# Growing the delta rule's triangular inverse in 32-row blocks instead of 64-row blocks, with the transposed copy made on VectorE

## Chip, cores and metric

The kernel runs on one core of a Trainium2 chip. The metric is the device time of one execution in microseconds (us), start to end; lower is better. Inputs and outputs are float32.

## What is computed

The reference is a two-layer mixer followed by two layers of a second kind. Each layer of the first kind has an attention branch and a gated delta rule branch; the change touches the delta rule alone:

```python
def chunked_gated_delta_rule(q, k, v, beta, g):
    ...
    lower = jnp.where(strict, jnp.einsum('bhnid,bhnjd->bhnij', kb, k) * decay, 0.0)
    tmat = jnp.eye(CHUNK, dtype=jnp.float32) + lower
    u = lax.linalg.triangular_solve(tmat, v * beta[..., None], left_side=True,
                                    lower=True, unit_diagonal=True)
    w = lax.linalg.triangular_solve(tmat, kb * jnp.exp(gc)[..., None], left_side=True,
                                    lower=True, unit_diagonal=True)
    ...
```

With 8 heads, 256 positions and 128 columns per head, each layer solves with unit lower triangular matrices I + L. The kernel uses blocks of 128 positions, so there are 2 x 8 matrices of 128x128 in a layer, and it computes their inverses explicitly.

## The kernel before

All five engines run one static program. A list of steps, `PLAN`, is merged from several lanes by the string `ORDER` (L319): one letter takes the next step of that lane. Lane `a` holds the delta rule's chain, `b` the attention chain, `m` the big matrix products, `s` the loading and splitting of weights, and others hold drains and tails. Every engine goes through `PLAN` from the front and does its part of each step, so `ORDER` fixes the order of work on each engine; semaphores make a step wait for its inputs.

The bulk of the work are products with weights (`mm`, L941, L926, L934): a weight unit of 512 KB comes in by DMA, ScalarE rounds it to a high part (`w_hi`, L1347), GpSimd subtracts to get the low part (`w_lo`, L866, L868), and TensorE forms three products. One unit of two K blocks is 12 matmuls of 128x512. Steps of the chains stand between such units on TensorE, and their results go to two PSUM buffers `chain`, used in turn; a step that takes a buffer waits until the step before the last has been emptied.

The delta rule runs in two groups `g` of four heads in each layer, so four inverses of 8 matrices each (2 row blocks, 4 heads) are made in a run. In each:

- `rep` (TensorE, L1053) and `sub` (VectorE, L1958 to L1973) invert the 8x8 diagonal blocks and write them, transposed, into 64-wide rows of `xth`.
- `x1` (TensorE, through `half_blocks`, L970) transposes them by products with the identity, and ScalarE copies the result into `xh`. Both the inverse so far (`xh`) and its transpose (`xth`) are kept.
- For each of the levels 8, 16, 32: `invY` multiplies with L (16 matmuls of 64x64x64, L970), VectorE masks the result (L1999); `invZ` forms the correction and, as a second product, its transpose (32 matmuls, L970), and VectorE subtracts the one from `xh` (L2006, step `invZ`) and the other from `xth` (L2015, or L2018 and L2019 at the last of the three, step `invX`).
- Level 64 joins the two 64-row halves: 8 matmuls (L1080), a copy (L1996), 8 matmuls (L1095), a subtraction (L2009).
- `vT` turns the values (8 transposes, L962); it stands behind `invZ` of the first level and is independent of the inverse. `raw` (L1143) and `iT` (L962) are steps of the attention chain.

The matmuls of the first three levels come in pairs, one on rows 0 to 63 and one on rows 64 to 127 of the array:

```python
for j in range(R * 4):
    for at in halves:
        a, b = pair(j, at)
        m = pe.matmul(c[at, col + j * HALF:col + (j + 1) * HALF], a, b, ...)
```

The trace shows two matmul instructions for each such float32 matmul, so the 160 of an inverse are 320 instructions, and 1280 in the run. All of a product's results lie in one PSUM bank, 512 float32 per partition.

Of the kernel before, what the change touches and what calls it, by code (L numbers as in the profile page):

```python
# [29 lines left out]
P = 128  # L30
# [23 lines left out]
HALF = P // 2  # L54
K_ID, K_TRIU, K_LEVEL, K_BLOCK, K_NEG, K_STR, K_NSTR, K_TRIL, K_ONE, K_FREQ, K_UNIT, K_LATER, K_HALF, K_OWN = (
    0, 128, 256, 448, 576, 832, 1088, 1344, 1472, 1600, 1640, 1648, 1776, 1777)
K_COLS = K_OWN + HALF


def shape_constants():  # L60
# [5 lines left out]
    own = HALF * (p // HALF) + f[:, 0:HALF]  # L66
    for n, s in enumerate(LEVELS[:-1]):
        c[:, K_LEVEL + n * HALF:K_LEVEL + (n + 1) * HALF] = (
            (p // (2 * s) == own // (2 * s)) & (p // s % 2 == 1) & (own // s % 2 == 0))
    c[:, K_BLOCK:K_BLOCK + P] = p // BLK == f // BLK  # L70
    c[:, K_OWN:K_OWN + HALF] = p // BLK == own // BLK
# [163 lines left out]
def gdn_chain(g):  # L235
    out = [("stat", 0, g), ("stat", 1, g), ("rn", g), ("avT", g),
           ("dec", g, 0), ("dec_b", g, 0), ("dec_c", g, 0), ("kk", g, 0), ("dec", g, 1), ("dec_b", g, 1),
           ("dec_c", g, 1), ("kk", g, 1), ("rep", g), ("sub", g), ("x1", g)]
    for n in range(len(LEVELS)):
# [4 lines left out]
        if n < len(LEVELS) - 1:  # L244
            out.append(("invX", g, n))
        if n == 0:
            out.append(("vT", g))
# [51 lines left out]
def lanes():  # L299
# [20 lines left out]
    "aaaaasammssvamsmssaamaaasaacsccasscccssammcmmsmaacssmmaacssccsmmmamaaasasmdabsmaaabssmmcsmaammassdbm"  # L320
    "adbmssaaammsssammsbadamsabaamamsaaaamssacmasccmaamasbsbbmacccscmammssmsccsaacbcmmbssmambbsaaasssammb"
    "bdsaaaamsssdmmmmaassdwbbssmmmsamcbmmamssssbbdbbmmaaambabxxsasbmaabbbsddmxssbaamswwamaaamaassmamsdwaa"
    "mwbasxsxmmsdmsaxbmwxsaxxxbmbbmxaxvsvsssmssmmmammsmaammsdsaaammsssssvammmmaaaascasscmmsccasscmcassccm"
    "msmaammcmsacsmcasmsassdaaaammasassmmaambbsmambacmaaamdassmssbdbssmaamabammaaamssaaadmsscamacsmssssaa"
    "mmamccacccmssbbscbcmmcamssacammbbsssmabbsmaaamdssaaaammssdsammadmmaabbscbbbmaswmmssdsbbbaassmsssmaaw"
    "maabmmbambsbxmxxbmssdbbbmmsssdamawammaasaadswwmbamasxxbsamaamssbaxdbbwxsxxmmmxxxsssssvsmmsvasadmmmmm"
    "mmsaaaasassaassmmdsssssdssbsdsbbmmmmmmsmmmmammmmsssaassdaasmmbbsaadbbsmmmbsaaasmmbddabbmbbmssaaamvba"
    "bmbsssddmmbbadmmsssybbmbssbmaambdsymsbamdsyyavbymbysydvvmmyssdmvssvvvvdmsvvvdmmmmssdymmmmmmvvvssssss"
    "yvvsmmmmmmmvmmmvsseeessvvvvaeeessmmaaammmbmmmmmmssdmssssssssdmmmmmadsasmsbaaammmbbbaassdasssdbbmbmma"
    "asaamsbmbsddbmbbmaaabmsssvbbmbasmmsabbdmbddsssasmabbssmymmambayddssmbsmbdsssydvyysmsdbsyyvvmmydmmmmv"  # L330
    "svsmdvvvvmsvvyssssmmvvvmmyvvmvvmssemmmmmsseemmvvvveemmme"
# [3 lines left out]
def plan():  # L335
# [17 lines left out]
    "kk": "vector", "rep": "vector", "x1": "scalar", "kT": "vector", "invY": "vector", "invZ": "vector", "vT": "vector",  # L353
# [13 lines left out]
def emptied_by(step, *args):  # L367

    if step == "invZ" and args[-1] < len(LEVELS) - 1:
        return "invX"  # L370
    return EMPTIED_BY.get(step, step)
# [96 lines left out]
def build(nc, t, out):  # L468
    ctx = ExitStack()
    with ctx:  # L470
# [68 lines left out]
        xh, yh, xth = xx8[:, :, 0:HALF], yy8[:, :, 0:HALF], yy8[:, :, HALF:P]  # L539
# [336 lines left out]
        def _(pe):  # L876
            def handlers(p):
# [1589 lines left out]
```

## Time and profile before

| | |
|---|---|
| median of 3 runs | 1063.06 us (1062.7 to 1064.39) |
| span of the profiled execution, first to last instruction | 1056.6 us |
| the profiled execution's own time | not listed apart; the three runs lie 6.1 to 7.8 us above the span |
| TensorE busy | 1025.6 us, 97% of the span, 7112 matmuls |
| VectorE, ScalarE, GpSimd busy | 57%, 55%, 67% |
| bytes moved | 151.59 MB, 143 GB/s on the mean |

The page says for each engine how long it was busy, and for the 40 slices of the span how busy. The views by line give the duration of an operation, the views of waits tell which engine stood still for which, and the chain that ended last tells in order of time which work set the end. A matmul's end is modelled and matmuls overlap, so what one costs is read from the distance of starts, or from groups of different length.

### The profile page before, as it was taken

Reading aid. Unit: us, or ns where it says so; the run is one execution under the profiler, and the core shown is the slowest. Engines: PE = TensorE matmul, PEld = TensorE weight load, DVE = VectorE, ACT = ScalarE, POOL = GpSimd, SP = SyncE. Lnnn points to the kernel's source line nnn. Section 1 sums busy time; section 2 is a strip of 40 time slices with the busy share of each in tenths; the row PEclk is TensorE's granted clock in tenths of the full one; section 3 lists DMA queues with packets and bytes.
Section 4 is the critical chain, followed back from the end, with each engine's and each line's share of the span. In section 5 each row is a group of like instructions: output and inputs, shape, how many; then the busy total and the mean of one; then the engine's idle time right before and its main releaser. Section 6 shows DMA issues by size and latency. Waiting matters only on the chain.

```text
span 1056.6 us, 18561 instructions
## 1 busy us (share of the span) xinstructions
PE 1025.6 (97%) x7112; PEld 886.4 (84%) x7112; DVE 599.0 (57%) x1181; ACT 577.4 (55%) x968; POOL 712.2 (67%) x550
## 2 busy tenths in 40 slices
PE   8999999999999999999999998999999989999986
PEld 8988998888877988899888887788888768888875
DVE  4774366786565557246584563517446560646564
ACT  4754347656644574336656744445576534567652
POOL 4786537872648787556766645897366978744794
PEclk9999999999999999999999999999999999999999
DMA  8664434653425555435444332665233546423451
GB/s 294 192 179 122 139 101 131 173 156 107 134 100 153 180 165 157 140 84 157 141 139 141 115 125 87 209 191 158 81 113 120 186 140 216 133 91 108 140 183 57
DMA packets 80584, 151.59 MB, mean 143 GB/s; under 512 B 6448, under 2 KB 12400, under 8 KB 80496
## 3 DMA queue, kind: packets, MB, share of 16 engines
q1 hardware_dynamic: 80496, 150.41, 46.9%
q8 instruction: 57, 0.93, 0.4%
q14 instruction: 31, 0.25, 0.1%
HBM read 149.34 MB, written 1.05 MB: 142 GB/s over the span
## 4 chain that ended last, share of the span: by engine, by line
PE 88%; DVE 4%; ACT 3%; POOL 3%; issue 2%; DMA 0%; POOLq 0%; SPq 0%; DVEq 0%; ACTq 0%
PE bulk L941 53%; PE bulk L926 12%; PE chain L962 5%; PE chain L970 4%; PE chain L1039 4%; PE chain L1307 1%; PE bulk L934 1%; PE chain L1288 1%; ACT arena L1347 1%; PE chain L1163 1%; PE chain L1179 1%; POOL w_lo L868 1%; DVE arena L1846 1%; PE chain L1030 1%; POOL w_lo L866 1%
## 5 line engine op out<-in xcount | busy, mean ns | idle before, releaser
L866 POOL TENSOR_TENSOR w_lo<-raw,w_hi 128x512 fp32r<-128x512 f32 (+3 forms) x259 | 340.7, 1316 | 292.4 <-ACT w_hi L1347 291.8
L868 POOL TENSOR_TENSOR w_lo<-raw,w_hi 128x512 fp32r<-128x512 f32 (+3 forms) x277 | 375.6, 1357 | 31.8 <-ACT w_hi L1347 31.8
L1347 ACT ACTIVATE w_hi<-raw 128x1024 fp32r<-128x1024 f32 (+4 forms) x277 | 277.3, 1019 | 210.1 <-PE bulk L941 163.4
L941 PE MATMUL bulk<-w_hi,hT_hi 128*128 128x512 f32 (+1 forms) x756 | 306.0, 405 | 0.8 <-ACT arena L1347 0.5
L941 PE MATMUL bulk<-w_hi,hT_lo 128*128 128x512 f32 (+1 forms) x756 | 294.4, 389 | 0.0
L941 PE MATMUL bulk<-w_lo,hT_hi 128*128 128x512 f32 (+1 forms) x756 | 204.2, 389 | 1.9 <-POOL w_lo L868 1.9
L941 PEld LDWEIGHTS bulk<-w_hi,hT_hi 128*128 128x128 f32 x756 | 142.4, 188 | 33.5 <-issue 1.9
L941 PEld LDWEIGHTS bulk<-w_lo,hT_hi 128*128 128x128 f32 x756 | 141.7, 188 | 32.7 <-POOL w_lo L868 3.4
L941 PEld LDWEIGHTS bulk<-w_hi,hT_lo 128*128 128x128 f32 x756 | 142.5, 188 | 26.8 <-issue 1.0
L926 PE MATMUL bulk<-hT_hi,w_hi 128*128 128x256 f32 x384 | 96.3, 289 | 0.0
L926 PE MATMUL bulk<-hT_lo,w_hi 128*128 128x256 f32 x384 | 94.0, 282 | 0.0
L962 PE MATMUL chain<-cst,arena 128*128 128x128 f32 (+1 forms) x544 | 73.4, 276 | 7.8 <-DVE arena L2223 3.5
L962 PEld LDWEIGHTS chain<-cst,arena 128*128 128x128 f32 (+1 forms) x544 | 62.7, 142 | 15.1 <-issue 9.3
L926 PEld LDWEIGHTS bulk<-hT_hi,w_hi 128*128 128x128 f32 x384 | 73.4, 191 | 0.9 <-ACT w_hi L1347 0.7
L1347 ACT ACTIVATE arena<-chain 128x512 f32<-128x512 f32 (+4 forms) x64 | 45.5, 727 | 52.0 <-PE chain L962 23.6
L926 PEld LDWEIGHTS bulk<-hT_lo,w_hi 128*128 128x128 f32 x384 | 73.5, 191 | 0.0
L1846 DVE SCALAR_TENSOR_TENSOR arena<-bulk,par,arena 128x253 f32<-128x253 f32 (+2 forms) x144 | 59.4, 475 | 21.0 <-ACT arena L1347 19.0
L1342 ACT ACT_TABLE_LOAD x44 | 56.5, 1283 | 26.5 <-PE bulk L941 14.3
L1347 ACT ACTIVATE arena<-bulk 128x1024 f32<-128x1024 f32 (+2 forms) x50 | 50.1, 1006 | 17.3 <-PE bulk L941 17.2
L926 PE MATMUL bulk<-hT_hi,w_lo 128*128 128x256 f32 x384 | 53.9, 283 | 0.0
L1347 ACT ACTIVATE arena<-arena,tiny 128x256 f32<-128x256 f32 (+1 forms) x80 | 36.2, 454 | 27.0 <-DVE tiny L2345 19.4
L926 PEld LDWEIGHTS bulk<-hT_hi,w_lo 128*128 128x128 f32 x384 | 49.5, 192 | 0.0
(262 smaller groups left out, 1393.4 us busy)
## 6 DMA issues: line engine op xcount, KB each, us to landing
raw<-in_w_in_dram SPq DMA_DIRECT2D x194, 512.0 KB, 3.6
raw<-in_w_out_dram SPq DMA_DIRECT2D x32, 512.0 KB, 3.7
raw<-in_w_branch_dram SPq DMA_DIRECT2D x16, 512.0 KB, 3.7
raw<-in_w_mem_kv_dram SPq DMA_DIRECT2D x8, 512.0 KB, 3.4
raw<-in_w_merge_up_dram SPq DMA_DIRECT2D x16, 256.0 KB, 2.9
raw<-in_w_in_dram SPq DMA_DIRECT2D x8, 420.0 KB, 3.4
gain<-in_ln_rows_dram SPq DMA_DIRECT2D x4, 512.0 KB, 5.3
gain<-in_gains_dram SPq DMA_DIRECT2D x3, 512.0 KB, 6.1
```

Of the source, the lines that this page charges most:

```text
L866: pool.tensor_tensor(lo_of(p, u)[:, 0:at], raw_of(p, u)[:, 0:at], hi_of(p, u)[:, 0:at].bitcast(F32), ALU.subtract).then_inc(first_part, 1)
L868: pool.tensor_tensor(lo_of(p, u)[:, at:n], raw_of(p, u)[:, at:n], hi_of(p, u)[:, at:n].bitcast(F32), ALU.subtract).then_inc(p.done("split" ...
L926: m = pe.matmul(dst, part[:, k, j * P:(j + 1) * P], b[:, kk, :], start=(not low and kk == 0 and i == 0 and j % 2 == 0), stop=(low and kk = ...
L934: m = pe.matmul(pair[0:n, 0:S], part[:, k, :], b[:, kk, :], start=(not low and kk == 0 and i == 0), stop=(low and kk == tot - 1))
L941: m = pe.matmul(dst, a, part[:, k, :], start=(first and not low and k == 0 and i == 0), stop=(last and low and k == nk - 1))
L962: m = pe.transpose(c[0:n, i * P:i * P + v.shape[0]], v, ident[0:v.shape[0], 0:v.shape[0]])
L970: m = pe.matmul(c[at, col + j * HALF:col + (j + 1) * HALF], a, b, start=(j == 0), stop=(j == R * 4 - 1), skip_group_check=True)
L1030: pe.matmul(c[:, j * P:(j + 1) * P], spread(4 * r + j, 8), rows_T[0:8, :], start=(j == 0), stop=(j == 3), skip_group_check=True)
L1039: m = pe.matmul(c[:, j * P:(j + 1) * P], a, b, start=(j == 0), stop=(j == 3), skip_group_check=True)
L1342: act.preload_act_table_set(sets[func])
L1347: return act.activation(dst, src, func, **more)
L1846: ins = STT(cv[:, j, back:S], b[:, j * S:(j + 1) * S - back], par1[:, p.l, c:c + 1], cv[:, j, back:S], ALU.mult, ALU.add)
```

## The change

The inverse now grows in 32-row blocks up to level 32, and the transposed copy comes from VectorE:

- `half_blocks` becomes `quad_blocks`: for each of the 8 matrices four matmuls of 32x32x32 on the four 32-row blocks of the array. All results lie in one bank as before, 32 columns for each matrix (256 in all, not 512).
- `sub` writes 32-wide rows with one operation for all 8 matrices, and VectorE's transpose of 32x32 blocks makes the other copy. `x1` is gone from TensorE and ScalarE.
- At levels 8 and 16, `invZ` forms one product; VectorE subtracts, and then transposes the result (`invX`).
- A new VectorE step `place` spreads the 32-row blocks into the 128-wide and 64-wide matrices, zero elsewhere, by two multiplications with a mask.
- Level 32 is now a joining step: the tiles take their weights from one 32-row block and write the neighbouring one; both products are formed, and VectorE writes them with the sign changed. Level 64 is as before.
- `ORDER` is another string (as many letters). Loads, splits and all other products are the same steps in another order.

```diff
-                def half_blocks(c, pair, col=0):
+                def quad_blocks(c, pair, to=0, col=0):
 
                     for j in range(R * 4):
-                        for at in halves:
-                            a, b = pair(j, at)
-                            m = pe.matmul(c[at, col + j * HALF:col + (j + 1) * HALF], a, b, start=(j == 0), stop=(j == R * 4 - 1),
+                        for i in range(4):
+                            at, dst = quads[i], quads[i ^ to]
+                            a, b = pair(j, at, dst)
+                            m = pe.matmul(c[dst, col + j * QUAD:col + (j + 1) * QUAD], a, b, start=(j == 0), stop=(j == R * 4 - 1),
                                           skip_group_check=True)
...
-                def x1(g):
-                    c = take("x1", g)
-                    pe.wait_ge(*p.after("vector", "sub", g))
-                    half_blocks(c, lambda j, at: (xth[at, j, :], ident[at, at])).then_inc(p.done("x1"), 1)
...
-                    if n < len(LEVELS) - 1:
-                        half_blocks(c, lambda j, at: (lt8[at, j, at], xh[at, j, :])).then_inc(p.done("invY"), 1)
+                    if LEVELS[n] < QUAD:
+                        m = quad_blocks(c, lambda j, at, dst: (lt8[at, j, at], xq[at, j, :]))
+                    elif LEVELS[n] == QUAD:
+                        m = quad_blocks(c, lambda j, at, dst: (lt8[at, j, dst], xq[at, j, :]), to=1)
...
-                    if n < len(LEVELS) - 1:
-                        half_blocks(c, lambda j, at: (xth[at, j, :], yh[at, j, :]))
-                        half_blocks(c, lambda j, at: (yh[at, j, :], xth[at, j, :]), 512).then_inc(p.done("invZ"), 1)
+                    if LEVELS[n] < HALF:
+                        m = quad_blocks(c, lambda j, at, dst: (xtq[at, j, :], yq[at, j, :]))
+                        if LEVELS[n] == QUAD:
+                            m = quad_blocks(c, lambda j, at, dst: (yq[at, j, :], xtq[at, j, :]), to=1, col=512)
...
-                    for r in range(R):
-                        for j in range(4):
-                            ins = TT(xth[:, 4 * r + j, :].rearrange("p (b i) -> p b i", i=BLK),
-                                     over(inv[:, 4 * r + j, :], HALF // BLK), blocks, ALU.mult)
-                    ins.then_inc(p.done("sub"), 1)
+                    TT(xtq_flat.rearrange("p (m b i) -> p m b i", m=R * 4, i=BLK), inv[:, :, :].unsqueeze(2).broadcast_to(dims),
+                       blocks.unsqueeze(1).broadcast_to(dims), ALU.mult).then_inc(p.own, 1)
+                    v.wait_ge(*p.last())
+                    v.transpose(xq_flat, xtq_flat).then_inc(p.done("sub"), 1)
...
+                    if LEVELS[n] < QUAD:
+                        v.transpose(xtq_flat, xq_flat).then_inc(p.done("invX"), 1)
...
+                def place(g):
+
+                    own = cst[:, K_QUAD:K_QUAD + 4]
+                    for dst, src, n, at in ((xt8, xtq, 4, slice(0, P)), (xh, xq, 2, halves[0])):
+                        dims = [at.stop, R * 4, n, QUAD]
+                        ins = TT(dst[at, :, :].rearrange("p m (b n) -> p m b n", b=n), src[at, :, :].unsqueeze(2).broadcast_to(dims),
+                                 own[at, 0:n].unsqueeze(1).unsqueeze(3).broadcast_to(dims), ALU.mult)
+                    ins.then_inc(p.done("place"), 1)
```

In layer 0, group 0, TensorE had this order from `x1` to `invZ` of the first level (`iT`'s 5 transposes and `vT`'s 8 are L962; the leading rows of bulk units are left out):

```order
L970 MATMUL chain<-cst,arena 64x64 x16
...
L970 MATMUL chain<-arena 64x64 x16
L962 MATMUL chain<-cst,arena 128x128 x5
...
L941 MATMUL bulk<-w_lo,hT_hi 128x512 x4
L970 MATMUL chain<-arena 64x64 x32
L962 MATMUL chain<-cst,arena 128x128 x8
L941 MATMUL bulk<-w_hi,hT_hi 128x512
```

At the same place it now has `invY`, one bulk unit, `invZ`, `vT` and at once `invY` of the second level:

```order
L980 MATMUL chain<-arena 32x32 x32
L950 MATMUL bulk<-w_hi,hT_hi 128x512
...
L950 MATMUL bulk<-w_lo,hT_hi 128x512 x4
L980 MATMUL chain<-arena 32x32 x32
L971 MATMUL chain<-cst,arena 128x128 x8
L980 MATMUL chain<-arena 32x32 x32
```

`x1` is gone, the second product of `invZ` is gone, and between `invZ` and the next `invY` only `vT`'s 8 transposes are left, where two bulk units stood behind them.

On VectorE, in the same inverse, the first two levels and the start of the third were (L1986 drains `vT`):

```order
L1999 TENSOR_TENSOR arena<-chain,cst 128x8x64
L2006 TENSOR_TENSOR arena<-arena,chain 128x8x64
L2015 TENSOR_TENSOR arena<-arena,chain 128x8x64
L1986 TENSOR_TENSOR arena<-chain,tiny 128x512 x2
L1999 TENSOR_TENSOR arena<-chain,cst 128x8x64
```

and are now:

```order
L2006 TENSOR_TENSOR arena<-chain,cst 128x256
L2013 TENSOR_TENSOR arena<-arena,chain 128x256
L2024 STREAM_TRANSPOSE arena<-arena 128x256
L1991 TENSOR_TENSOR arena<-chain,tiny 128x512 x2
...
L2036 TENSOR_TENSOR arena<-arena,cst 128x1024
L2036 TENSOR_TENSOR arena<-arena,cst 64x512
L2003 COPY arena<-chain 128x256
```

The subtraction of the second copy became a transpose of half the columns, and `place` (L2036) stands between the second and third level, once in each inverse.

## Rows read from the trace of the kernel before

**Rows 1.** The page: busy time of each engine; granted TensorE clock in 40 slices.
```profile
PE 1025.6 (97%) x7112; PEld 886.4 (84%) x7112; DVE 599.0 (57%) x1181; ACT 577.4 (55%) x968; POOL 712.2 (67%) x550
...
PEclk9999999999999999999999999999999999999999
```

**Rows 2.** Windows: stretch, length, busy time by engine, clock, DMA share, GB/s.
```profile
core 0: us, PE busy (x) PEld busy (x) DVE busy (x) ACT busy (x) POOL busy (x), PEclk, DMA share, GB/s
50.00:150.00 100.00, 99.98 (x916) 87.52 (x914) 52.96 (x138) 44.97 (x74) 63.40 (x51) 1.00 0.47 138
516.00:636.00 120.00, 118.57 (x918) 100.53 (x917) 77.88 (x165) 71.72 (x125) 76.13 (x58) 1.00 0.45 132
```

**Rows 3.** Waits: who waited for whom, us in total, times, longest; ScalarE, GpSimd, TensorE.
```profile
POOL w_lo L866 <- ACT w_hi L1347: 291.8, 110, 13.0
ACT w_hi L1347 <- PE bulk L941: 163.4, 102, 5.3
...
PE chain L962 <- DVE arena L2223: 3.5, 2, 2.9
```

**Rows 4.** The chain that ended last, 86 to 120 us: start, us, what, instructions.
```profile
87.81 1.08 PE chain L970 x32
88.89 2.95 PE bulk L941 x12
...
96.36 2.01 PE chain L970 x64
98.37 1.02 PE chain L962 x8
99.40 5.48 PE bulk L941 x24
...
118.34 1.09 PE chain L1143 x16
```

**Rows 5.** TensorE's timeline: 64-row tiles in pairs (L970) and one alone (L1080).
```profile
112.11 2.08 PE L970 MATMUL chain<-arena 64*64 64x64 f32 x64
117.19 1.15 PE L970 MATMUL chain<-arena 64*64 64x64 f32 x32
...
124.51 1.11 PE L1080 MATMUL chain<-arena 64*64 64x64 f32 x16
```

**Rows 6.** TensorE's timeline: pairs of 8-row tiles with 128 columns.
```profile
63.59 0.27 PE L1030 MATMUL chain<-arena,cst 8*128 8x128 f32 x1
63.60 0.27 PE L1032 MATMUL chain<-arena,cst 8*128 8x128 f32 x1
63.70 0.27 PE L1030 MATMUL chain<-arena,cst 8*128 8x128 f32 x1
```

**Rows 7.** Groups by line, VectorE: shapes xcount, busy us, mean ns, idle before.
```profile
L2223 DVE TENSOR_TENSOR arena<-arena 128x1024 f32<-128x1024 f32 x4 | 5.9, 1466 | 0.5
L1999 DVE TENSOR_TENSOR arena<-chain,cst 128x512 f32<-128x512 f32 x12 | 8.3, 692 | 26.4 <-PE chain L970 26.3
L2242 DVE CUSTOM_DVE_ANT_0 arena<-arena 128x384 f32<-128x384 f32 (+1 forms) x8 | 7.9, 1041 | 58.6 <-ACT arena L1347 58.6
L2353 DVE TENSOR_TENSOR arena<-chain,tiny 128x256 f32<-128x256 f32 x12 | 5.1, 424 | 0.4
L2351 DVE RECIPROCAL tiny<-tiny 128x4 f32<-128x4 f32 x12 | 2.1, 178 | 28.6 <-PE chain L1307 28.5
```

**Rows 8.** VectorE's timeline in `sub` of layer 0, group 0: first and last operations.
```profile
82.47 0.22 DVE L1965 TENSOR_TENSOR chain<-chain,tiny 128x56 f32<-128x56 f32 x1 [2.07 <-PE chain L1053]
...
85.46 0.17 DVE L1968 TENSOR_TENSOR tiny<-tiny,chain 128x8 f32<-128x8 f32 x1
85.66 1.29 DVE L1973 TENSOR_TENSOR arena<-tiny,cst 128x64 f32<-128x64 f32 x8
```

**Rows 9.** VectorE's timeline: the handover from TensorE to `invZ`'s subtraction.
```profile
98.49 0.69 DVE L2006 TENSOR_TENSOR arena<-arena,chain 128x512 f32<-128x512 f32 x1 [4.76 <-PE chain L970]
```

**Rows 10.** Groups by line: ScalarE's table loads, GpSimd's second half of a split.
```profile
L868 POOL TENSOR_TENSOR w_lo<-raw,w_hi 128x512 fp32r<-128x512 f32 (+3 forms) x277 | 375.6, 1357 | 31.8 <-ACT w_hi L1347 31.8
...
L1342 ACT ACT_TABLE_LOAD x44 | 56.5, 1283 | 26.5 <-PE bulk L941 14.3
```

More of the change, by code:

```diff
@@ L237, in gdn_chain @@
            ("dec", g, 0), ("dec_b", g, 0), ("dec_c", g, 0), ("kk", g, 0), ("dec", g, 1), ("dec_b", g, 1),
-           ("dec_c", g, 1), ("kk", g, 1), ("rep", g), ("sub", g), ("x1", g)]
+           ("dec_c", g, 1), ("kk", g, 1), ("rep", g), ("sub", g)]
     for n in range(len(LEVELS)):
@@ L245, in gdn_chain @@
             out.append(("invX", g, n))
+        if LEVELS[n] == QUAD // 2:
+            out.append(("place", g))
         if n == 0:
@@ L319 @@
 ORDER = (
[L320 to L329, printed above, removed]
@@ L352 @@
     "baT": "vector", "memT": "vector", "cwT": "vector", "hT": "vector", "gc": "vector", "stat": "scalar", "dec": "vector", "avT": "scalar",
-    "kk": "vector", "rep": "vector", "x1": "scalar", "kT": "vector", "invY": "vector", "invZ": "vector", "vT": "vector",
+    "kk": "vector", "rep": "vector", "kT": "vector", "invY": "vector", "invZ": "vector", "vT": "vector",
     "kq": "vector", "u": "scalar", "st": "scalar", "ks": "vector", "o": "vector", "iT": "scalar",
@@ L367, in emptied_by @@
 def emptied_by(step, *args):
-    if step == "invZ" and args[-1] < len(LEVELS) - 1:
+    if step == "invZ" and LEVELS[args[-1]] == QUAD:
         return "invX"
@@ L538, in build @@
         lt8 = lt[:, :, :, :].rearrange("p r j n -> p (r j) n")
-        xh, yh, xth = xx8[:, :, 0:HALF], yy8[:, :, 0:HALF], yy8[:, :, HALF:P]
+        quads = [slice(i * QUAD, (i + 1) * QUAD) for i in range(4)]
+        xf, yf = [t[:, :, :].rearrange("p m n -> p (m n)") for t in (xx8, yy8)]
+        xh, yh = [t[:, 0:512].rearrange("p (m n) -> p m n", n=HALF) for t in (xf, yf)]
+        xq_flat, xtq_flat, yq_flat = xf[:, 768:1024], yf[:, 512:768], yf[:, 768:1024]
+        xq, xtq, yq = [t.rearrange("p (m n) -> p m n", n=QUAD) for t in (xq_flat, xtq_flat, yq_flat)]
         rhs = xx[:, 0, :, :].rearrange("p j n -> p (j n)")
@@ L1071, in invY @@
                     if n == 0:
-                        pe.wait_ge(*p.after("scalar", "x1", g))
+                        pe.wait_ge(*p.after("vector", "sub", g))
                     else:
@@ L1081, in invY @@
                                           stop=(j == R * 4 - 1), skip_group_check=True)
-                        m.then_inc(p.done("invY"), 1)
+                    m.then_inc(p.done("invY"), 1)
                 def invZ(g, n):
@@ L1096, in invZ @@
                                           stop=(j == R * 4 - 1), skip_group_check=True)
-                        m.then_inc(p.done("invZ"), 1)
+                    m.then_inc(p.done("invZ"), 1)
                 def kq(g, r):
@@ L1515, in dec_b @@
                     A(dt_[:, r, :, :], dt_[:, r, :, :], ACT.Exp).then_inc(p.done("dec_b"), 1)
-                def x1(g):
-                    act.wait_ge(*p.after("tensor", "x1", g))
-                    A(xh, heads(half("x1", g)[:, 0:R * 4 * HALF], R * 4), ACT.Copy).then_inc(p.done("x1"), 1)
                 def half(*key):
@@ L2020, in invX @@
+                    if LEVELS[n] < QUAD:
+                        v.transpose(xtq_flat, xq_flat).then_inc(p.done("invX"), 1)
+                    else:
+                        for i in (2, 0):
+                            ins = TS(xt8[quads[i], :, quads[i + 1]], heads(c[quads[i], 512:768], R * 4), -1.0, None, ALU.mult)
+                        ins.then_inc(p.done("invX"), 1)
                     v.wait_ge(*p.here("invX"))
+                def place(g):
[5 more added lines that the diff above has]
+                    ins.then_inc(p.done("place"), 1)
+                    v.wait_ge(*p.here("place"))
@@ L2424, in handlers @@
                             norm_c=norm_c, hT=hT, drain_v=drain, gmul=gmul, tap=tap, tap_on=tap_on, ba_a=ba_a, ba_c=ba_c, gc=gc_, stat=stat, rn=rn,
-                            dec=dec, dec_c=dec_c, kk=kk, rep=rep, sub=sub, kT=kT, vT=vT, invY=invY, invZ=invZ, invX=invX, kq=kq, ks=ks, o=o_,
+                            dec=dec, dec_c=dec_c, kk=kk, rep=rep, sub=sub, kT=kT, vT=vT, invY=invY, invZ=invZ, invX=invX, place=place, kq=kq, ks=ks, o=o_,
                             onorm_a=onorm_a, onorm_c=onorm, zgain=zgain, kinorm_a=kinorm_a, rope_i=rope_i, raw=raw_, topk=topk,
```

63 lines of the change are left out of this document (38 added, 25 removed).

## Prediction

> **What bounds the kernel now.** I first read the page's busy times: TensorE is busy 97% of the span, VectorE, ScalarE and GpSimd 55 to 67%, and the granted TensorE clock stands at full speed in every slice [rows 1]. A share over the whole span can hide stages, so I then read windows around the inverses: in 50 to 150 us TensorE is busy 99.98 of 100.00 us at clock 1.00, while VectorE, ScalarE and GpSimd have 53, 45 and 63; in 516 to 636 us, the last inverse's stretch, 118.57 of 120.00 [rows 2]. The waits say the same from the other side: ScalarE waits 163.4 us for matmuls to free a weight slot and GpSimd 291.8 us for ScalarE, while TensorE's own longest wait is 3.5 us in total [rows 3]. The weight pipeline is ahead; TensorE is behind nobody. So here a microsecond of TensorE work removed is a microsecond of run time, as long as the new order finds no new wait. The chain that ended last agrees: around the first inverse it is bulk products and the inverse's own groups, end to end on TensorE [rows 4].
>
> **What a tile costs now.** On that chain a group of 32 instructions of 64x64 tiles takes 1.08 us and one of 64 takes 2.01 [rows 4]. The 32 more, 16 pairs, cost 0.93 us: 58 ns a pair, and 1.08 - 16 x 0.058 = 0.15 us is fixed for a group. That the two tiles of a pair run at once is seen by comparing with one tile alone: 16 instructions on a single 64x64 tile take 1.11 us, 32 in pairs 1.15 [rows 5]. The second tile is all but free. Two instructions on different row strips start 0.01 us apart, and their pairs with 128 moving columns follow each other in 0.11 us [rows 6]; with 64 columns it was 0.058. That is (0.11 - 0.058) / 64 = 0.8 ns a column, and so 32 columns should take 58 - 32 x 0.8 = 32 ns.
>
> **What goes and comes on TensorE, for one inverse.** Before: `x1` 1.08, and three levels of 1.08 + 2.01, together 10.35 us. (Level 64 stays.) After: four tiles for each of 8 matrices, two instructions each, make 64 instructions or 16 rounds of four in each of five groups, and 128 or 32 rounds in the last `invZ`. If four tiles run at once as two do now, a round costs the 32 ns above: five groups of 0.15 + 16 x 0.032 = 0.66, one of 0.15 + 32 x 0.032 = 1.17, together 4.48 us. The difference is 5.87 us, in four inverses 23.5.
>
> `x1` also took a switch: the 12 bulk matmuls behind a group take 2.95 us, while 24 in one stretch take 5.48, 2.74 for 12 [rows 4]. Four switches less, 0.2 us each, give 0.8. **Sum: 24.3 us.**
>
> The price of four tiles at once is the one that no row shows. Its floor is the streaming alone, 32 x 0.8 = 26 ns a round: 4 x (10.35 - 0.9 - 112 x 0.026) + 0.8 = 27.0 us gained. Its ceiling is one tile at a time at the mean distance of today's instructions, 29 ns: 448 x 0.029 + 0.9 = 13.9 us an inverse, 3.5 more than now. I take 32 ns, since the nearest row is the pair, whose second tile costs nothing.
>
> All four tiles of a round write one PSUM bank, on different partitions. Today's pairs do this too, and run at once [rows 5]. The Trainium skill ("TensorEngine Tiling", Restrictions and Gotchas) says that different row tiles cannot access the same PSUM bank at the same time; by that rule the rounds would be serial, the ceiling above, and the run slower. The pairs contradict it for two tiles, so I leave it a rival's chance and not the forecast.
>
> **The other engines.** `x1`'s copy leaves ScalarE; it gets five table loads more (49 in the program, 44 before) at 1.28 us [rows 10], 6.4 us in all, covered by its 163.4 us of waiting for TensorE [rows 3]. Loads and splits are the same in number; GpSimd's longest half of a split, 1.36 us [rows 10], and its 63 to 76 us of work in the two windows [rows 2] stay under TensorE's time even if 12 us leave each layer.
>
> VectorE's masks and subtractions shrink from 512 to 256 columns, 0.69 to about 0.42 us [rows 7]. The 32x32 transpose has no row: between the smallest operation (0.18) and the custom one over 384 columns (1.04) [rows 7]; I take the 0.42 of a 256-column operation. `place` is 1024 columns from SBUF, 1.47 us [rows 7], and 512 more at some 0.7, about 2.2 us. The sum for an inverse hardly moves: ten operations of some 0.69 (6.9 us) and 1.29 in `sub` go; eight of 0.42, three transposes at the same price, one operation of some 0.5 in `sub` and `place` come, 7.3 us. VectorE has 42 to 47 us free in each window [rows 2], so I count none of it, provided TensorE doesn't wait for it. Where would it? At three places the cover is short.
>
> - `sub` to `invY`: from `rep`'s end VectorE takes 82.47 to 85.63, then wrote 64-wide rows in 1.29 [rows 8]; now one operation and a transpose, about 1.0. TensorE has two bulk units there (5.48 [rows 4]) against 0.12 + 3.2 + 1.0; even a transpose of 1.04 us fits.
> - `invZ` to `invY` of level 16 in group 0 of both layers: only `vT`'s 8 transposes stand between, 1.02 us [rows 4]. VectorE starts 0.12 us after the matmuls (98.37 to 98.49 [rows 4, 9]) and needs 0.42; with as much again for the way back 0.66. At the old 0.69 it would be 0.93. `invY` needs only the subtraction; the transpose is needed by `invZ`, one bulk unit later.
> - `invY` to `invZ` at level 32: only `raw`, 1.09 us [rows 4], against the same 0.66.
>
> So these are covered by 0.4 us; if all four of the last two kinds were 1 us late, 4 us would be lost. `place` comes two bulk units before its first reader on TensorE. Behind it on VectorE stands level 32's copy; between `invZ` of level 16 and the product that this copy empties, TensorE has at least a bulk unit (2.74) and five transposes, against 0.12 + 0.42 + 0.42 + 2.2 us on VectorE.
>
> The new `ORDER` moves other steps too. TensorE stands still 1056.6 - 1025.6 = 31 us in all [rows 1]; a better or worse merge can move a few of these. I allow 3 us either way and nothing in the sum.
>
> **Rivals.**
> 1. *Four tiles do not run at once, only two do.* Then 224 rounds of 32 ns: 8.07 us an inverse, a gain of 4 x 2.28 + 0.8 = 9.9 us, 1053 us. For it: no row has more than two tiles in flight. Against: starts 0.01 us apart [rows 6] leave room for four in 32 ns.
> 2. *TensorE takes the tiles one at a time (slower).* There are more instructions now: 448 in place of 320 in an inverse. If each costs the 29 ns that an instruction in a pair costs on the mean, an inverse takes 3.55 us more, the run 4 x 3.55 - 0.8 = 13.4 more: 1076.5. It decides from 21.5 ns an instruction (86 ns a round) on, where 448 of them fill the old 10.55 - 0.9 us. For it: no row sustains more than one matmul in 29 ns; short starts are seen in pairs alone. Against: pair and single tile take the same time [rows 5], so 29 ns is streaming, not a limit on issue. The skill ("TensorE: Matmul & The Clock Gate", Wait — 56ns, not 53.3ns?) says that matmuls never start closer than about 25 ns however few their columns; by that figure, as an estimate, an inverse would take 12.1 us and the run 1069. Starts 0.01 us apart [rows 6] speak against it for different tiles, but not for a long row of them.
> 3. *The time comes back as waits*: the shorter groups leave less cover, and VectorE answers late at more places than the four above. With half of the gain lost: 1051. For it: VectorE's queue holds other chains' work between the steps. Against: before, with longer operations, TensorE waited nowhere for the inverse [rows 3].
>
> **How the numbers follow.** Forecast: 1063.06 - 24.3 = 1038.8 us. The sum is made on an execution whose span is 1056.6, so 1032 is expected for the new span, with the same 6.5 us around it as at the median. Chances: forecast 0.62 (1036 to 1042 by the price of a round and the order), rival 1 0.17, rival 2 0.12, rival 3 0.09. A difference under 0.2%, 2.1 us, is about what a measurement cannot tell from none. Faster: 0.62 + 0.17 + most of rival 3 = 0.86; slower 0.12; same 0.02. The range reaches from 1033 (floor price, and 3 us from the order) to 1056 (rival 1 with 3 us lost), which leaves out rival 2.
>
> **What would show it.** Right: TensorE's groups of 32x32 tiles of 64 instructions take 0.6 to 0.7 us on the chain and those of 128 about 1.2; TensorE's busy time falls by some 24 us and its share stays near 97%; the transposes of 128x256 take 0.4 to 0.5 us and nothing of TensorE waits for them. Rival 1 would show 1.2 us for 64 instructions, rival 2 about 2.0, rival 3 short groups but new waits of TensorE for VectorE. A gain with groups longer than 0.9 us would mean that my reason is wrong and the order brought it.

## The result and the profile after

The change takes **1107.03 us** (median of 4 runs, 1105.39 to 1110.23), the kernel before 1062.88 on the same chip: ratio 1.0422, 95% interval 1.0389 to 1.0454. It is 4% slower; the forecast was 1038.8 us and the range ended at 1056. All ratios here use the runs within 1.5% of a kernel's fastest; of the one with GpSimd in pieces of 256 columns (below) two runs of four lie above that, the profiled one among them.

The page of the changed kernel, busy times, granted clock and the shares of the chain that ended last:

```profile
PE 1027.1 (93%) x7624; PEld 877.1 (79%) x7624; DVE 652.9 (59%) x1165; ACT 581.9 (53%) x969; POOL 723.0 (66%) x550
...
PEclk9998999999989999899899999999999999999999
...
PE 66%; DVE 21%; ACT 6%; issue 4%; POOL 2%; DMA 0%; POOLq 0%; DVEq 0%; SPq 0%; ACTq 0%
```

The shares of the chain before:

```profile
PE 88%; DVE 4%; ACT 3%; POOL 3%; issue 2%; DMA 0%; POOLq 0%; SPq 0%; DVEq 0%; ACTq 0%
```

Against [rows 1] TensorE's share fell from 97 to 93%, the clock is no longer full in every slice, and VectorE's busy time rose by 54 us although its operations got fewer and shorter. TensorE stands still 1103.9 - 1027.1 = 76.8 us, before 31.0. The clock records of the trace hold 56.2 us at a granted clock of 0.50 (the 1.2 GHz level), before 8.8. In 44.0 us of these TensorE was busy, before in 3.1; the rest lies in its waits or after its last matmul. Half of the busy part is lost, as an estimate: 22.0 against 1.6 us. The span grew by 47.3 = 45.8 standing + 20.4 clock - 18.9, so some 19 us of TensorE's work did go (24.3 were forecast); it was paid back three and a half times.

The chain that ended last, 105 to 127 us (start, us, what, instructions; L980 are the 32x32 tiles):

```profile
105.63 0.44 DVE arena L2006
...
106.20 0.74 PE chain L980 x48
...
112.99 0.68 PE chain L980 x50
113.68 2.95 PE bulk L950 x12
...
122.26 0.95 PE chain L980 x66
```

A group of 64 instructions takes 0.68 us at full clock, as forecast (0.66; the chain counts 50 of the 64 that the timeline has at 112.92 and 120.42), against 2.01 for 64 instructions of the old tiles [rows 4]. The tiles are not the trouble. But VectorE now has 21% of this chain, before 4%; around the first inverse TensorE had it end to end [rows 4]. TensorE's waits (us in total, times, longest):

```profile
PE chain L971 <- DVE arena L2242: 8.2, 2, 5.9
PE chain L971 <- DVE arena L1918: 7.3, 3, 5.1
PE chain L971 <- DVE arena L2387: 7.2, 2, 4.4
PE chain L971 <- DVE arena L2141: 5.1, 1, 5.1
...
PE bulk L950 <- POOL w_lo L877: 4.6, 7, 0.7
...
PE chain L980 <- DVE arena L2006: 1.7, 1, 1.7
```

None of the first four is a step that the new arithmetic touched: L2242 ends `mix`, L1918 ends the norm, L2387 and L2141 end two rotations (`rope_2` and `rope_i`). All are transposes (L971) waiting for VectorE, where the longest such wait was 3.5 us in total [rows 3].

One of them (L2141) in full. VectorE's timeline of the change before 446.42 us (start, us, operation):

```profile
433.03 1.60 DVE L1977 TENSOR_TENSOR arena<-tiny,cst 128x256 f32<-128x256 f32 x1
434.67 0.45 DVE L1980 STREAM_TRANSPOSE arena<-arena 128x256 f32<-128x256 f32 x1
...
438.03 1.29 DVE L2123 TENSOR_TENSOR arena<-arena,cos_t 128x144 f32<-128x144 f32 x1
439.25 1.39 DVE L2123 TENSOR_TENSOR arena<-arena,sin_t 128x144 f32<-128x144 f32 x1
...
443.26 1.25 DVE L2126 TENSOR_TENSOR arena<-arena 128x144 f32<-128x144 f32 x1
444.44 1.36 DVE L2127 TENSOR_TENSOR arena<-arena 128x144 f32<-128x144 f32 x1
```

GpSimd's timeline beside it:

```profile
433.06 1.29 POOL L875 TENSOR_TENSOR w_lo<-raw,w_hi 128x512 fp32r<-128x512 f32 x1
...
437.79 1.38 POOL L875 TENSOR_TENSOR w_lo<-raw,w_hi 128x512 fp32r<-128x512 f32 x1 [2.00 <-ACT w_hi L1356]
439.12 1.36 POOL L877 TENSOR_TENSOR w_lo<-raw,w_hi 128x512 fp32r<-128x512 f32 x1
440.44 1.34 POOL L875 TENSOR_TENSOR w_lo<-raw,w_hi 128x512 fp32r<-128x512 f32 x1
...
444.31 1.32 POOL L877 TENSOR_TENSOR w_lo<-raw,w_hi 128x512 fp32r<-128x512 f32 x1
```

and TensorE's:

```profile
446.42 1.30 PE L971 MATMUL chain<-cst,arena 128*128 128x128 f32 x5 [5.15 <-DVE arena L2141]
```

The same six operations of the rotation (`rope`, L2104 to L2108 there) in the kernel before, first and last, and GpSimd's work around them:

```profile
88.29 0.31 DVE L2104 TENSOR_TENSOR arena<-arena,cos_t 128x144 f32<-128x144 f32 x1
...
89.52 0.30 DVE L2108 TENSOR_TENSOR arena<-arena 128x144 f32<-128x144 f32 x1
```

```profile
84.64 1.29 POOL L868 TENSOR_TENSOR w_lo<-raw,w_hi 128x512 fp32r<-128x512 f32 x1
90.63 1.30 POOL L866 TENSOR_TENSOR w_lo<-raw,w_hi 128x512 fp32r<-128x512 f32 x1 [4.70 <-ACT w_hi L1347]
```

Before, GpSimd paused from 85.93 to 90.63 and each operation took 0.30 us. Now GpSimd's subtractions lie beside them one after the other and each takes 1.25 to 1.39, one GpSimd operation's time: 7.8 us for six in place of 1.5. Where the delay sits can be read off 433.03: alone this operation takes 0.42 us (the shortest of its kind), so its own work began at 434.63 - 0.42 = 434.21, 0.14 before GpSimd's operation ended at 434.35. In the 13 longest delays of the change it is 0.13 to 0.15. The VectorE operation waits for a GpSimd operation to end.

It need not be the first one. The longest delay of the change lasted until the third of GpSimd's operations beside it was nearly over:

```profile
690.72 4.09 DVE L1743 CUSTOM_DVE_ANT_0 arena<-xs 128x1024 f32<-128x1024 f32 x1 [0.17 <-DVE xs L1784]
```

```profile
689.90 1.35 POOL L877 TENSOR_TENSOR w_lo<-raw,w_hi 128x512 fp32r<-128x512 f32 x1
691.15 1.33 POOL L875 TENSOR_TENSOR w_lo<-raw,w_hi 128x512 fp32r<-128x512 f32 x1
692.41 1.32 POOL L877 TENSOR_TENSOR w_lo<-raw,w_hi 128x512 fp32r<-128x512 f32 x1
```

Alone it takes 1.21, so its own work began at 693.60, 0.13 before the last of them ended at 693.73.

The price of the clock is seen in windows around that wait (stretch, length, busy time of PE, PEld, DVE, ACT, POOL, granted clock, DMA share, GB/s):

```profile
435.00:441.30 6.30, 6.04 (x25) 4.16 (x23) 5.55 (x15) 4.16 (x6) 4.29 (x4) 1.00 0.44 145
441.30:446.40 5.10, 0.00 (x0) 0.01 (x1) 4.90 (x7) 0.00 (x0) 4.33 (x4) 0.91 0.71 205
446.40:452.30 5.90, 5.88 (x78) 4.73 (x79) 0.42 (x1) 4.05 (x5) 0.33 (x1) 0.50 0.31 92
```

TensorE stood still for 5.1 us and came back at clock 0.50 for 5.9 us; so this wait cost its length and some 3 us behind it.

Which VectorE operations suffer? Three lines of the change: count, shortest/median/longest in ns, first and last start in us:

```profile
L2226 DVE SCALAR_TENSOR_TENSOR arena<-arena,tiny x32: 335/344/1387, 295.7 to 671.1; 128x128 f32<-128x128 f32 x32
```

```profile
L2045 DVE SCALAR_TENSOR_TENSOR arena<-arena,tiny,chain x32: 339/342/348, 138.1 to 633.9; 128x128 f32<-128x128 f32 x32
```

```profile
L2364 DVE TENSOR_SCALAR tiny<-tiny x12: 169/320/1252, 777.7 to 1019.6; 128x4 f32<-128x4 f32 x12
```

The same operation on as many columns reaches 1387 ns where both tensors come from SBUF (L2226; 11 of the 13 that had GpSimd beside them were delayed) and never passes 348 where one is in PSUM (`chain`, L2045), though GpSimd worked beside 17 of those 32. A multiplication of 4 columns can take 1252. The Trainium skill ("SBUF — State Buffer", Who interferes with whom) states this: a VectorE instruction with two SBUF inputs, or one such as `tensor_scalar` that can run in a two-port mode, contends with a GpSimd instruction that reads SBUF, and whichever issues second is blocked until the first is done. On which operations are held up the trace agrees, with the numbers above. On how long, the trace decides otherwise: the VectorE operation at 690.72 came after two of GpSimd's that began 0.43 and 1.69 us behind it. I had not weighed any of this.

### The profile page after: what moved, and what is told of

Read it like the earlier page. It is cut to its first block, busy times and chain, and to the rows that moved or that the text cites. A ratio compares the mean times of both kernels' runs of the same rounds, so it can differ in the third digit from the quotient of the medians.

```text
span 1103.9 us, 19568 instructions
## 1 busy us (share of the span) xinstructions
PE 1027.1 (93%) x7624; PEld 877.1 (79%) x7624; DVE 652.9 (59%) x1165; ACT 581.9 (53%) x969; POOL 723.0 (66%) x550
## 4 chain that ended last, share of the span: by engine, by line
PE 66%; DVE 21%; ACT 6%; issue 4%; POOL 2%; DMA 0%; POOLq 0%; DVEq 0%; SPq 0%; ACTq 0%
PE bulk L950 37%; PE bulk L935 11%; PE chain L971 5%; PE chain L1049 3%; ACT arena L1356 2%; DVE arena L2123 2%; ACT L1351 1%; DVE arena L2226 1%; PE chain L1316 1%; PE chain L980 1%; POOL w_lo L877 1%; DVE arena L1758 1%; PE chain L1040 1%; POOL w_lo L875 1%; PE chain L1188 1%
## 5 line engine op out<-in xcount | busy, mean ns | idle before, releaser
L875 POOL TENSOR_TENSOR w_lo<-raw,w_hi 128x512 fp32r<-128x512 f32 (+3 forms) x259 | 347.9, 1343 | 324.6 <-ACT w_hi L1356 324.2
L877 POOL TENSOR_TENSOR w_lo<-raw,w_hi 128x512 fp32r<-128x512 f32 (+3 forms) x277 | 379.7, 1372 | 36.0 <-ACT w_hi L1356 36.0
L950 PE MATMUL bulk<-w_hi,hT_hi 128*128 128x512 f32 (+1 forms) x756 | 312.5, 413 | 4.1 <-issue 3.3
L950 PE MATMUL bulk<-w_hi,hT_lo 128*128 128x512 f32 (+1 forms) x756 | 301.2, 398 | 0.0
L950 PE MATMUL bulk<-w_lo,hT_hi 128*128 128x512 f32 (+1 forms) x756 | 207.6, 393 | 4.6 <-POOL w_lo L877 4.6
L950 PEld LDWEIGHTS bulk<-w_hi,hT_hi 128*128 128x128 f32 x756 | 146.5, 194 | 37.3 <-issue 5.8
L950 PEld LDWEIGHTS bulk<-w_hi,hT_lo 128*128 128x128 f32 x756 | 146.9, 194 | 28.5 <-issue 1.0
L971 PE MATMUL chain<-cst,arena 128*128 128x128 f32 (+1 forms) x544 | 77.5, 287 | 36.4 <-DVE arena L2242 8.2
L971 PEld LDWEIGHTS chain<-cst,arena 128*128 128x128 f32 (+1 forms) x544 | 64.9, 147 | 46.9 <-issue 38.1
L1356 ACT ACTIVATE arena<-chain 128x512 f32<-128x512 f32 (+4 forms) x60 | 43.1, 734 | 75.5 <-PE chain L971 45.5
L1356 ACT ACTIVATE arena<-arena 128x128 f32<-128x128 f32 (+3 forms) x65 | 37.8, 584 | 31.4 <-DVE arena L1929 13.4
```

Source lines behind the costliest of these rows:

```text
L875: pool.tensor_tensor(lo_of(p, u)[:, 0:at], raw_of(p, u)[:, 0:at], hi_of(p, u)[:, 0:at].bitcast(F32), ALU.subtract).then_inc(first_part, 1)
L877: pool.tensor_tensor(lo_of(p, u)[:, at:n], raw_of(p, u)[:, at:n], hi_of(p, u)[:, at:n].bitcast(F32), ALU.subtract).then_inc(p.done("split" ...
L950: m = pe.matmul(dst, a, part[:, k, :], start=(first and not low and k == 0 and i == 0), stop=(last and low and k == nk - 1))
L971: m = pe.transpose(c[0:n, i * P:i * P + v.shape[0]], v, ident[0:v.shape[0], 0:v.shape[0]])
L1356: return act.activation(dst, src, func, **more)
```

## The experiments

To compare all kernels by one number, I sum for every VectorE operation its time beyond the shortest of its own line and shape: **E**, VectorE's time lost to company. Before, it is 64.1 us (77 operations over 0.2 us), in the change 113.5 (125). This is a lower bound, since a line whose every operation met GpSimd has no undisturbed one: measured from the shortest in the run with short GpSimd below, the change has 143. Ratios are to the kernel before on the same chip.

| kernel | us | ratio, 95% interval | E, us |
|---|---|---|---|
| new arithmetic, old order | 1050.2 | 0.9889 [0.9848, 0.9931] | 69.5 |
| old arithmetic, new order | 1139.78 | 1.0746 [1.0702, 1.0789] | 107.1 |
| the change, GpSimd short | 1021.75 | 0.9634 [0.9596, 0.9672] | 6.9 |
| before, GpSimd short | 1051.85 | 0.9911 [0.9886, 0.9937] | 4.9 |
| new arithmetic, old order, GpSimd short | 1033.12 | 0.9733 [0.9712, 0.9754] | 4.6 |
| old arithmetic, new order, GpSimd short | 1075.58 | 1.0143 [1.0114, 1.0171] | 6.7 |
| the change, GpSimd in pieces of 256 | 1110.22 | 1.038 [1.0319, 1.0441] | 111.0 |
| the change, stepped pieces of 256 | 1123.88 | 1.0584 [1.0534, 1.0633] | 51.1 |
| the change, stepped in the first part only | 1091.2 | 1.0288 [1.0241, 1.0336] | 71.2 |
| new arithmetic, old order, merged `mix_b`, stepped | 1108.22 | 1.0425 [1.0386, 1.0464] | 46.1 |
| the change, merged `mix_b` | 1106.92 | 1.0437 [1.0403, 1.0471] | 113.5 |
| new arithmetic, old order, merged `mix_b` | 1048.1 | 0.9873 [0.9853, 0.9894] | 68.9 |

**Arithmetic or order?** First the new arithmetic with the string `ORDER` of before, `x1`'s letters dropped and `place` right behind `invX` of level 16; then the reverse, `x1` right behind `sub`:

```diff
-    "aasaaaammssvssaaassmmsmaaaaacccmmmmmsscssacmmscccaassaamsammccmsscasmaaaacssmabssaammmddsammbamasmss"
+    "aaaaasammssvamsmssaamaaasaacsccasscccssammcmmsmaacssmmaacssccsmmmamaaasasmdabsmaaabssmmcsmaammssdbma"
...
```

> The changed inverse in the order of the kernel before (its steps keep their places; x1 falls out, place stands directly behind invX of level 16). Theory O (the new merge of the lanes costs the time, the arithmetic saves it): 1063 less the 18 to 24 us of TensorE work, 1039 to 1045 us, granted clock back at 0.99 or more. Theory A (the 32-row tiles, transposes or place cost the time): slower than 1080. Theory C in its strong form (VectorE's operations collide with GpSimd's whenever the timing is not the one the order was made for): 1050 to 1080, with VectorE's busy time above 630 us.

> The inverse of the kernel before in the order of the change (place falls out, x1 stands directly behind sub). Theory O: about as slow as the change plus what the arithmetic had saved and the waits don't swallow, 1107 to 1130 us, TensorE's idle time above 60 us and clock below 0.985. Theory A: 1055 to 1070, as the kernel before.

1050.2 and 1139.78 us. Neither lies where I expected it: the first is 5 us above the range of theory O, and theory C, whose range it just touches, wanted VectorE busy for over 630 us, where it is 605.8; the second is above its range too. The arithmetic is worth some 11 us in the old order, the new order costs 79 us beside the old arithmetic. So the loss is the order's; E goes with it, 69.5 in the old order and 107.1 in the new. Not all of the 79 is the change's, though: TensorE's largest wait there, 18.9 us in total, is `x1` for `sub`, a step that the change does not have (see below).

**GpSimd or the order itself?** GpSimd subtracts 64 of every 512 columns, and the low parts of the other columns are left out:

```diff
-                    pool.tensor_tensor(lo_of(p, u)[:, at:n], raw_of(p, u)[:, at:n],
-                                       hi_of(p, u)[:, at:n].bitcast(F32), ALU.subtract).then_inc(p.done("split"), 1)
...
+                    pool.tensor_tensor(lo_of(p, u)[:, at:at + 64], raw_of(p, u)[:, at:at + 64],
+                                       hi_of(p, u)[:, at:at + 64].bitcast(F32), ALU.subtract).then_inc(p.done("split"), 1)
```

> The change, with GpSimd's subtraction done for 64 of every 512 columns only: the low parts of the weights are left out for the other columns (the slots are zeroed once at the start), so GpSimd is hardly ever at work beside VectorE. Theory C (VectorE's operations on SBUF wait for the GpSimd operation beside them, and TensorE waits for VectorE): VectorE's busy time falls from 653 to below 590 us, the run to 1035 to 1060. Theory O without C (the links are too short whatever GpSimd does): 1090 to 1107, and VectorE's busy time hardly moves.

> The same shortening in the kernel before, as a control (the low parts of the weights are left out for seven eighths of the columns). Theory C and theory O: a small gain, 1050 to 1063 us, since TensorE waits little there; whatever it gains has to be taken off the gain of the change with the same shortening.

The change falls by 85 us to 1021.75, the kernel before by 9 to 1051.85. The page of the change with short GpSimd, and its rotation, the same as at 438.03 above:

```profile
PE 995.8 (98%) x7624; PEld 862.3 (85%) x7624; DVE 516.2 (51%) x1165; ACT 580.9 (57%) x969; POOL 185.1 (18%) x551
```

```profile
407.04 0.31 DVE L2125 TENSOR_TENSOR arena<-arena,cos_t 128x144 f32<-128x144 f32 x1
407.27 0.42 DVE L2125 TENSOR_TENSOR arena<-arena,sin_t 128x144 f32<-128x144 f32 x1
```

VectorE has 137 us less to do with the same instructions, TensorE is busy 98%, and the change beats the kernel before by 30 us. The time lies below theory C's range, 1035 to 1060 us. Short GpSimd also ends TensorE's waits for `w_lo`, but these were only 4.6 us in the change.

The other two corners:

> The new arithmetic in the order of before (run e1), with GpSimd subtracting only 64 of every 512 columns; the other low parts of the weights are left at zero, so the output lacks them. The fourth corner of arithmetic, order and GpSimd. If the order costs only through what GpSimd does to VectorE, this and the change with short GpSimd (1021.75 us) come out within 4 us of each other, at 1020 to 1028 us, and the gain of the arithmetic is then the forecast 24 to 30 us below 1051.85. If the new order costs or gains by itself, they differ by more.

> The old arithmetic in the new order (1139.8 us with GpSimd's full work), with GpSimd subtracting only 64 of every 512 columns; the other low parts of the weights are left at zero, so the output lacks them. It completes the table of arithmetic, order and GpSimd. If the new order costs only through VectorE's waits for GpSimd, this comes within 8 us of the old order's 1051.85 us, most likely below it (with the new arithmetic the new order was 11 us better): 1040 to 1056. If the order has a cost of its own beside the old arithmetic, 1065 or more.

I expected the order to cost nothing by itself, and that was wrong both ways. With GpSimd short it gains 1.0% beside the new arithmetic (0.9634 against 0.9733) and loses 2.3% beside the old (1.0143 against 0.9911). Most of the loss is one wait, which neither the change nor the kernel before has:

```profile
PE chain L972 <- DVE arena L1975: 15.7, 4, 4.6
```

`x1` waits for `sub` four times, where I had put it, and the new order left no cover there. In all TensorE stands 14.6 us longer than in the kernel before with short GpSimd, and loses some 12 us to the clock. What GpSimd's full work costs in ratio: 0.009 before, 0.016 in the new arithmetic alone, 0.060 in the new order alone, 0.079 in the change. So with either arithmetic GpSimd's company costs the new order five to seven times as much as the old.

**Does a VectorE operation wait for the end of GpSimd's?** Then cutting GpSimd's operations in two should halve the delays.

```diff
+                    mid = (at + n) // 2
+                    piece(u, at, mid)
+                    piece(u, mid, n).then_inc(p.done("split"), 1)
```

> The change, whole, with every subtraction of 512 columns on GpSimd cut into two of 256. GpSimd then does the same work in twice the operations; from the rows of the runs so far (64 columns 0.35 us, 512 columns 1.35 us) one of 256 should take about 0.8 us, so that its total rises from 723 to about 835 us. Theory W (a VectorE operation that meets a GpSimd operation waits for about the rest of it): the small VectorE operations that met GpSimd fall with the length of GpSimd's operation, from the 1.0 to 1.4 us they take in the change (128x4 0.995, 128x128 of mix_b 1.217, 128x144 of rope up to 1.39) to 0.6 to 0.9. Theory S (the two share the memory's throughput, so that what counts is the columns GpSimd has still to do): they stay at 1.0 to 1.4 us. Of the time: by W 1065 to 1095 us unless GpSimd itself becomes late in the stretches of bulk products, and then TensorE's waits for w_lo say so; by S 1107 or more.

The half of this on the operations came out, the half on the time did not. The small operations that had GpSimd beside them fell, on the mean, as theory W says: 128x4 (L2364) from 0.995 to 0.452 us (below its 0.6 to 0.9), `mix_b`'s 128x128 from 1.217 to 0.764. But the time is not shown to differ from the change's, 1110.22 us (1096.78 to 1123.28). VectorE, GpSimd and TensorE's waits in the profiled execution (1114.1 us; the GpSimd rows are 25, 4 and 4 pieces):

```profile
1059.45 17.31 DVE L1837 TENSOR_TENSOR arena<-arena 128x1024 f32<-128x1024 f32 x1
```

```profile
1052.91 17.33 POOL L881 TENSOR_TENSOR w_lo<-raw,w_hi 128x256 fp32r<-128x256 f32 x25
1070.20 2.76 POOL L881 TENSOR_TENSOR hT_lo<-raw,hT_hi 128x256 fp32r<-128x256 f32 x4
1072.92 2.76 POOL L881 TENSOR_TENSOR sT_lo<-raw,sT_hi 128x256 fp32r<-128x256 f32 x4
```

```profile
PE bulk L954 <- issue: 36.2, 4, 15.9
```

An operation of 1.22 us lasted 17.31: its own work began at 1076.76 - 1.22 = 1075.54, 0.14 before the last of GpSimd's pieces without a gap ended at 1075.68. This happened twice. TensorE stood 15.9 us each time, and the clock records hold 17.1 us at half clock, of which it worked 5.4 and 3.5 us. Without these two stalls this run would take, as an estimate, 1114.1 - 2 x 15.9 - (5.4 + 3.5) / 2 = 1078 us, inside theory W's range. Whether the shorter runs had both stalls is not shown. So VectorE is not let in after one operation by right.

So each piece was made to wait for the end of the one before, which leaves a gap, mostly of 0.08 us:

```diff
+                def step(u, a, b):
+                    piece(u, a, b).then_inc(p.own, 1)
+                    pool.wait_ge(*p.last())
```

> The change with GpSimd's subtractions in pieces of 256 columns, as in the run with fine pieces, but each piece waits for the end of the piece before it, so that GpSimd leaves a short gap after every piece. In the run with fine pieces a VectorE operation of 1024 columns stood 17.3 us, twice, while 24 GpSimd pieces followed each other without a gap, and TensorE stood 15.9 us each time. If a VectorE operation is let in wherever GpSimd pauses, those two stalls and the half-clock stretches of 17 us behind them go, and no VectorE operation lasts over 0.8 us longer than alone: 1107 falls to 1062 to 1085 us, unless the gaps (about 1090 of them, at an estimated 0.06 to 0.1 us) make GpSimd late, in which case TensorE's waits for w_lo, 5.2 us in the run with fine pieces, grow to over 20 us. If a gap does not let VectorE in, the two stalls remain and the time stays above 1095 us.

> The new arithmetic in the order of before with the merged mix_b (1048.1 us), with the same stepped GpSimd pieces of 256 columns. With GpSimd cut short this order took 1033.1 us, with its full subtractions 1048 to 1050: halving the wait of each VectorE operation that meets GpSimd should give back about half of the 15 us between them, so 1038 to 1044 us, if GpSimd does not become late. If it does, 1050 or more, with TensorE's waits for w_lo (1.9 us now) over 8 us.

No VectorE operation is delayed by more than 0.59 us, and E falls (113.5 to 51.1, 68.9 to 46.1): the gap does let VectorE in. But both kernels are slower, for the reason named as the alternative. TensorE's waits in the stepped change (4.6 us without steps) and in the stepped old order (1.9 us without):

```profile
PE bulk L959 <- POOL w_lo L883: 40.7, 68, 1.8
```

```profile
PE bulk L959 <- POOL w_lo L883: 39.7, 69, 1.8
```

Four pieces of 0.79 us and their gaps take some 3.5 us for a weight unit, where TensorE needs 2.74 [rows 4]. GpSimd, covered until then, became the bound in the stretches of bulk products. Stepping only the weights up to the delta rule's end tells the two apart:

```diff
+                    fine = p.sec != "two"
...
+                    if fine:
+                        step(u, at, mid)
```

> The change with the stepped pieces of 256 columns only for the weights of the first two thirds of the program (up to about 650 us, where the delta rule is); the rest of the weights is subtracted in whole halves, as in the change. In the run stepped throughout TensorE waited 40.7 us for w_lo, some 29 us of it after 650 us, so that cost should go and about 10 us of it stay. If VectorE's waits for GpSimd are what the new order costs in the delta rule, the VectorE part of TensorE's idle time up to 650 us (about 28 us in the change) falls by half or more and the half-clock stretches there (37 us at half speed) go with it: 1080 to 1092 us. If the new order loses its time there for another reason, 1104 or more.

1091.2 us, at the upper end of the range. TensorE's waits for VectorE up to 650 us are 10.7 us, against 32.1 up to 660 in the change, and the half-clock records there 13.7 against 37.5. In the same wait view GpSimd's lateness is down, and of the first-part waits named above L2141's is no longer among the longest dozen, L1918's (now L1931) is 1.5, and `mix`'s (now L2255) fell from 8.2 to 5.1:

```profile
PE bulk L963 <- POOL w_lo L887: 16.1, 28, 1.5
PE chain L984 <- DVE arena L2400: 7.2, 2, 4.4
PE chain L984 <- DVE arena L2255: 5.1, 2, 2.9
...
PE chain L984 <- DVE arena L1931: 1.5, 2, 1.2
```

L2400 is L2387 above, in the part that was left as it was: still 7.2.

**Fewer collisions instead of shorter ones.** Eight products of 128 columns in each half of `mix_b` become two of 1024:

```diff
-                            ins = STT(g1[:, r, at], od[:, r, at], so[:, 1, r, j:j + 1], g1[:, r, at], ALU.mult, ALU.mult)
...
+                    TT(g1[:, :, cols], g1[:, :, cols], od[:, :, cols], ALU.mult).then_inc(p.own, 1)
+                    v.wait_ge(*p.last())
...
+                    TT(gh, gh, sh, ALU.mult).then_inc(p.done("mix_b"), 1)
```

> The change, with the eight VectorE multiplications of 128 columns that mix_b does per half turned into two of 1024 (first by od, then by so spread over 128 columns); same products, other order of rounding. Theory W (each operation that meets GpSimd costs about one of GpSimd's, whatever its size): the eight of 1.217 us (9.7 us a half) become two of about 2 us (4 us a half), the wait of TensorE for mix_b's chain (8.2 us of idle behind the last VectorE operation of it) shrinks to under 4 us, and the half-clock stretches behind it go: 1085 to 1100 us. If the number of operations is not what costs, the two take as long as the eight, and the time stays at 1104 to 1110 us.

> The new arithmetic in the order of before (run e1), with the merged mix_b, and the first group's inverse transposes of layer 0 placed behind one more bulk product. If TensorE's remaining waits in e1 (2.86 us behind the rotated lanes, 3.14 and 2.06 us behind mix) come from VectorE operations that meet GpSimd, the time falls from 1050.2 to 1040 to 1047 us. If they have another cause it stays within 1 us of 1050.

In the change the waits for `mix`, the longest of 5.9 us, went, and nothing was gained: 1106.92 us. E is 113.5 as before, the wait for L2006 grew from 1.7 to 4.7 us, and the clock records hold 66.0 us at half clock. The collisions moved elsewhere. How a fix at one place shifts the meetings at the next I did not settle. In the old order the merged version, in which `ORDER` also has two neighbouring letters exchanged, takes 1048.1 us, between the two outcomes that I had named; its interval overlaps that of 1050.2, so the merge is not shown to help. Both are below the kernel before, by 1.1 and 1.3%, and so below the change.

## Why the prediction was wrong

**The tiles: right.** 32 ns a round of four gave 0.66 us for a group of 64; it takes 0.68. 128 instructions of `invZ` at level 32 were forecast in one group of 1.17; on the chain above they stand in two parts of 0.95 and 0.45 with 1.69 us of "issue" between, which I cannot explain, but in the other three inverses they run through, 0.53 us longer than 64. That is 8.3 ns an instruction or 33 a round, where rival 2 needed 21.5 ns an instruction. TensorE's busy time falls by 26.8 us (1022.6 to 995.8) where GpSimd is short, and by 21.3 (to 1001.3) with the arithmetic alone; the forecast was 24.3. Rivals 1 and 2 fall, and with them the rule about one PSUM bank: four row tiles of a round write one bank, 64 instructions in 0.68 us, a round in hardly more than the 26 ns that one tile's streaming was priced at, and the rule (the Trainium skill, "TensorEngine Tiling", Restrictions and Gotchas) does not hold here.

**The step that failed** is the sentence "I allow 3 us either way and nothing in the sum" for the new `ORDER`. The order is worth 1.0% less time without GpSimd's company, and 5.3% more with it (1.0422 against 0.9889). I read the string as moving TensorE's work only; it also decides what stands beside VectorE's operations.

**Its root is in "the other engines".** There I priced VectorE from means: "0.42 of a 256-column operation", "about 2.2 us" for `place`, "about 1.0" for `sub`'s end, and held GpSimd to be covered since its work would "stay under TensorE's time". The change's groups (count, busy us, mean ns, idle before):

```profile
L2036 DVE TENSOR_TENSOR arena<-arena,cst 128x1024 f32<-128x1024 f32 x4 | 6.6, 1655 | 0.1
...
L2036 DVE TENSOR_TENSOR arena<-arena,cst 64x512 f32<-64x512 f32 x4 | 6.0, 1492 | 0.0
...
L1977 DVE TENSOR_TENSOR arena<-tiny,cst 128x256 f32<-128x256 f32 x4 | 5.1, 1282 | 0.1
```

`place` takes 3.15 us and `sub`'s end 1.28 + 0.45. The masks and subtractions of the inverse, which read PSUM, came in at the forecast 0.42. GpSimd does stay under TensorE's time; what it costs is VectorE's. A warning stood in the rows I used: a mean of 1466 ns for 1024 columns [rows 7], where 512 columns from PSUM take 692, is no price of an operation but a mixture: the line's four took 1224 to 1226 ns and, once, 2186.

**Rival 3** had the right form, "the time comes back as waits", and was dismissed since TensorE waited nowhere for the inverse [rows 3]. But that was true of the old order only, in which GpSimd happened to pause beside the rotation, `mix_b` and the norm: of the rotation's 16 products with cos and sin in the first two layers two had GpSimd beside them, in the change 15. That these run beside GpSimd now because their lanes lie next to more bulk products is my reading; no run took it apart. Rival 3 was priced at half the gain; the waits and the clock behind them cost 66.2 us. The clock was in no term: 20.4 us, nearly a third of the loss.

## What to carry to other kernels

Where VectorE and GpSimd both work, price a VectorE operation with its inputs in SBUF twice: alone, and with at least a GpSimd operation's length added. Ask of a new order what will stand beside each stage, not only whether each engine has time left. Read min/median/max of a line, since a mean hides two populations. Before shortening GpSimd's operations, check what its pauses are good for and whether it can afford them.

## What I had not expected of the chip

- VectorE's delay is not bounded by one GpSimd operation: an operation of 1.21 us stood 4.09 us in the change, and with pieces of 0.78 us and no gap one of 1.22 us stood 17.31. With a gap of some 0.08 us after each piece no delay passed 0.59 us. Why VectorE was let in between two pieces at some places and not at others is open.
- Cutting GpSimd's operation in two is not free: 128x512 took 1.35 to 1.38 us, 128x256 0.78. In a row, where they overlap a little, the first start every 1.25 us, the second every 0.70, so 1.39 for the same columns; GpSimd's busy time rose from 723.0 to 804.4 us.
- Waits of 1.7 to 5.9 us left TensorE at granted clock 0.50 for 3.4 to 10.2 us in the change; 12 bulk matmuls took 3.77 us there in part, 2.95 at full clock.
